# Second block's attention: the order in which differential and grouped pairs of a query tile are worked

## The reference, cut to what matters

```python
def _diff_attention(dq, dk, dv, lam):
    s = jnp.einsum('bqhjd,bkhjd->bhjqk', dq, dk).astype(jnp.float32) * ATTN_SCALE
    p = jax.nn.softmax(s, axis=-1)
    a = (p[:, :, 0] - lam * p[:, :, 1]).astype(dv.dtype)
    return jnp.einsum('bhqk,bkhe->bqhe', a, dv)

def _gqa_attention(gq, gk, gv):
    s = jnp.einsum('bqhgd,bkhd->bhgqk', gq, gk).astype(jnp.float32) * ATTN_SCALE
    p = jax.nn.softmax(s, axis=-1).astype(gv.dtype)
    return jnp.einsum('bhgqk,bkhd->bqhgd', p, gv)
```

## Time and profile before

| what | us |
|---|---|
| median of 3 runs | 4246.14 (4244.86 to 4246.96) |
| the profiled execution | 4247.18 |
| its span in the trace | 4245.3 |
| attention of layer 0 in the trace | from 1516 to 1711 |
| attention of layer 1 in the trace | from 3237 to 3397 |
| TensorE busy over the span | 3767.7 (89%) |
| VectorE, ScalarE, GpSimd busy over the span | 1764.2, 864.0, 1032.4 |

### The profile page before, as it was taken

The page is one execution under the profiler, slowest core; times in us unless marked ns, Lnnn a source line. Parts: engine busy times, 40 slices in busy tenths (PEclk is TensorE's granted clock), DMA queues, the critical chain, the costliest instruction groups (busy, mean ns, idle before and its releaser), DMA issues. The chain is left out here.

```text
span 4245.3 us, 46759 instructions
## 1 busy us (share of the span) xinstructions
PE 3767.7 (89%) x17898; PEld 2594.1 (61%) x17898; DVE 1764.2 (42%) x3243; ACT 864.0 (20%) x1654; POOL 1032.4 (24%) x866
## 2 busy tenths in 40 slices
PE   6967968777669989899998899999899989989998
PEld 5856735444455557555554455555687757767887
DVE  3345320000032256488643666654224635234345
ACT  2123320000031246211212100001223511221001
POOL 1301200000003410123332323232142024434443
PEclk9978989999879999999999999999999999999999
DMA  5430179999811100122221223221111012222221
GB/s 197 179 97 16 61 285 397 394 398 397 342 40 56 45 21 1 50 81 93 79 96 60 80 104 115 100 98 60 35 62 38 1 61 77 82 80 70 90 80 60
DMA packets 79787, 496.39 MB, mean 117 GB/s; under 512 B 9680, under 2 KB 11088, under 8 KB 25808
## 3 DMA queue, kind: packets, MB, share of 16 engines
q1 hardware_dynamic: 69920, 469.80, 29.7%
q0 software_dynamic: 3792, 12.85, 1.0%
q10 hardware_dynamic: 5856, 10.75, 0.7%
HBM read 476.58 MB, written 16.78 MB: 116 GB/s over the span
## 5 line engine op out<-in xcount | busy, mean ns | idle before, releaser
L1942 PE MATMUL ps<-expert_weights,experts_x_turned 128*64 128x256 f32 x2112 | 284.5, 430 | 89.7 <-DMA expert_weights<-w_moe 88.0
L1942 PEld LDWEIGHTS ps<-expert_weights,experts_x_turned 128*64 128x64 f32 x2112 | 199.4, 155 | 183.2 <-issue 127.7
L755 PE MATMUL ps<-projected,weight_ring 128*128 128x384 f32 (+1 forms) x672 | 245.8, 521 | 0.0
L2025 DVE TENSOR_TENSOR experts_hidden<-experts_silu_gate,ps 128x256 f32<-128x256 f32 x33 | 13.9, 421 | 493.0 <-PE ps L1942 493.0
L755 PEld LDWEIGHTS ps<-projected,weight_ring 128*128 128x128 f32 x672 | 127.7, 190 | 106.1 <-issue 45.9
L2952 PE MATMUL ps<-h2b,weight_ring 128*128 128x384 f32 (+1 forms) x512 | 153.5, 444 | 23.6 <-PEq L247 23.6
L1169 DVE TENSOR_REDUCE attention_shift<-ps 128x1 f32<-128x768 f32 (+1 forms) x160 | 130.9, 845 | 77.0 <-PE ps L1057 76.7
L2390 DVE SCALAR_TENSOR_TENSOR projected<-projected,sb_vectors 128x497 f32<-128x497 f32 (+26 forms) x270 | 157.8, 648 | 1.6
L1057 PE MATMUL ps<-projected 64*128 64x256 f32 (+1 forms) x576 | 135.8, 527 | 25.0 <-DVE projected L1198 15.0
L1908 POOL DMA_INDIRECT experts_gathered<-tokens,own_tokens x32 | 28.9, 902 | 517.9 <-PE ps L1930 455.4
L2250 PE MATMUL ps<-projected,gates_weight_sums 128*128 128x384 f32 (+1 forms) x512 | 149.1, 434 | 5.0 <-POOL gates_weight_sums L2530 5.0
(11 more groups left out here) (645 smaller groups left out, 7623.5 us busy)
## 6 DMA issues: line engine op xcount, KB each, us to landing
weight_ring<-w_stream SPq DMA_DIRECT2D x218, 1024.0 KB, 5.1
expert_weights<-w_moe SPq DMA_DIRECT2D x198, 1024.0 KB, 27.6
slot_out<-experts_down_out ACTq DMA_DIRECT2D x66, 128.0 KB, 7.5
weight_ring<-w_stream SPq DMA_DIRECT2D x16, 512.0 KB, 3.7
weight_ring<-w_stream SPq DMA_DIRECT2D x16, 384.0 KB, 3.1
slot_out<-sb_constants SPq DMA_DIRECT2D x15, 256.0 KB, 5.0
sb_x_all<-xT SPq DMA_DIRECT2D x1, 3072.0 KB, 12.2
tokens<-h_tokens ACTq DMA_DIRECT2D x4, 512.0 KB, 4.6
```

Of the source, the lines that this page charges most:

```text
L755: ins = nc.tensor.matmul(core.ps[:, 2 * slot + half, 0:n], w_of(k), h_of(k)[:, a:a + n], start=(first and k == 0), stop=(last and k == chu ...
L1942: ins = nc.tensor.matmul(out[OWN * j:OWN * (j + 1), :], x_t[:, k, :], w[j][:, k, :], start=(k == 0), stop=(k == KD - 1), skip_group_check= ...
```

## The change

One line is taken out: the second `for c in range(4):`. The body of the second loop now stands in the first, so that the list holds differential 0, grouped 0, differential 1, grouped 1, and so on, in place of four of one kind and then four of the other.

```diff
                     for c in range(4):
                         pairs.append({
                             "maps": [(pr[r:r + HD, DQ + c, q], pr[r:r + HD, DK + c, :]) for r in (0, HD)],
                             "diff": True, "keys": keys, "spans": [(0, keys)],
                             "v": lambda i, c=c: dv[:, i, c * P:(c + 1) * P],
                             "out": pr[:, DQ + c, q]})
-                    for c in range(4):
                         pairs.append({
                             "maps": [(pr[r:r + HD, GQ + c, q], pr[r:r + HD, GK + c // 2, :])
                                      for r in (0, HD)],
                             "diff": False, "keys": keys, "spans": [(0, keys)],
```

## The result

The changed kernel takes **4261.69 us** (median of 9 runs, 4252.91 to 4264.94) against 4246.96 us for the kernel before in the same session (9 runs, 4239.38 to 4249.96). The ratio is 1.0031, with a 95% interval of 1.002 to 1.0041. The change makes the kernel slower by about 0.3%. The forecast was 4252.2 with a range that ended at 4257.2, so the time lies above the range.

A forecast was written before the change was run, and what follows sets the result against it. TensorE's own chain was taken to set the pace in the long pairs. Layer 1's +2.9 and layer 0's +3.2 gave +6.1 us, hence 4252.2 us, with a range of 4246.7 to 4257.2.

The forecast's parts named there:

- Start of a layer: First pairs of each layer's attention: T0 of pair 1 waits for a copy, +1.4 us in layer 1, +1.0 in layer 0.
- The link itself: Layer 0's start: T0 of pair 1 waits for the copy of pair 0's T, taken as +1.0 us.
- layer 1: start: T0 of layer 1's pair 1 waits for the copy of pair 0's T: +1.4 us, between 0.7 and 2.3.
- layer 1: long tiles: Alternating long pairs in layer 1: two pairs take 9.60 us, +1.2 a layer, between 0.8 and 1.9.
- layer 1: end: Layer 1's last pairs: T of differential pair 30 waits for its mix uncovered, +0.3 us, between -0.2 and +0.6.
- layer 0: start: Layer 0's first short pairs: the same wait for a copy, with less to copy, +1.0 us, between 0 and 1.4.
- layer 0: seam short to long: Layer 0, first long pairs: T0 of the grouped pair waits for a copy, +0.7 us, between 0.3 and 0.8.
- layer 0: short tiles: Layer 0's 16 short pairs: alternation taken as 0, with 1.6 us either way.
- The alternation fills the waits: Long tiles: rival in which TensorE's 0.47 us waits go, 15.0 us saved, 4237.2 us; chance 0.04.
- VectorE becomes the bound: Steps with two copies and a mix: rival in which VectorE's scale comes late, some 4260 us; chance 0.11.
- ring: Long tiles: one differential and one grouped pair repeat on TensorE, 9.60 us for the two.
- Nothing to be seen: Whole kernel: rival in which changes to and from `gv` cost nothing and starts are hidden, 4246.1 us; chance 0.07.

The follow-up runs named there:

- filled: Matmuls of the identity, results unread, added at the start of each layer's attention; on the kernel before 4250.91 and 4247.74 us, against 4246.89 and 4246.57 without.
- the first tile alone: Alternation only in layer 0's first short tile, against the kernel before: 4254.67 against 4249.08 us, again 4253.38 against 4246.57.
- the three comparisons: The whole change against the kernel before, measured three times: 4261.69 against 4246.96 us, 4256.84 against 4248.26, 4258.16 against 4249.08.
- the crossed runs: Alternation in layer 0's first tile without (4253.38 us) and with extra start matmuls (4248.94), beside the kernel before (4247.74) and the change (4255.52), both with them.
- the filled change: The full alternation with extra identity matmuls at each layer's start, against the kernel before without them: 4252.25 against 4246.89 us, again 4255.52 against 4246.57.
- the filled kernel before: The order of before with extra identity matmuls at each layer's start, against the kernel before without them: 4250.91 against 4246.89 us, again 4247.74 against 4246.57.
- two and two: Two differential then two grouped pairs in all tiles, against the kernel before: 4245.95 against 4246.89 us, ratio 0.9994.
- the long tiles of layer 0 alone: Alternation only in the four long tiles of layer 0, against the kernel before: 4248.04 against 4248.26 us, ratio 0.9999.

## Why the prediction was wrong

**The step that failed is "Start of a layer", the sentence "Layer 0 starts with short pairs, with less to copy: I take +1.0, between 0 and 1.4".** The link itself was right: filled, the first tile's alternation costs 0.75 in the trace (197.07 - 196.32) and 1.6 +- 0.8 in the runs. But the prediction held the length of the low stretch fixed. It looked at the granted clock at layer 1's start only, where it asked what one T0 would cost at the lower level, and put the clock aside with "the granted clock in the long pairs is full already". For the short pairs at layer 0's start no row of the clock was read at all. There the alternation does not only run under a given low clock, it goes with a longer stretch of it. In full: the wait for the copy was taken as the whole cost of the start, and the clock under which all the pairs after it run was put at nothing. As measured, the first tile alone costs 6.0 +- 0.8 in place of 1.0, so the term was too small by about 5. With 5 more the sum would have been 11.1, near the +10.6 +- 0.9 that the three comparisons give together.

Some of the miss in the number is chance. The first comparison, +13.0, was the highest of the three; +10.6 on 4246.14 would be 4256.7, just inside the range that ended at 4257.2. But the range reached so far only by adding up all its upper bounds, and the bound of this term was 1.4. Of a slowdown beyond 8.5 us the prediction said 0.13, nearly all of it for a late VectorE, which no trace shows.

Does the sum now close? The three comparisons of the change with the kernel before gave +13.0 +- 1.9 (the result), +9.7 +- 1.1 and +10.6 +- 2.3, weighted +10.6 +- 0.9. The links at the full clock give 5.7 by the traces, and what the first tile costs beyond its link is 6.0 - 0.75 = 5.2 +- 0.8 by the runs: 10.9. The whole is met within its error, the split less well. That 4.4 +- 1.1 of the first tile's 6.0 goes away with the extra work, under which the clock is full, is shown by the crossed runs. That the low stretch carries all of it is not, since 7 us more of it, by the clocks of all executions, are worth about 2. The two stages of the three traces of the changed order lie 6.1, 9.6 and 5.5 us above those of before, 7.1 on average and not 10.6. And the sum leaves out layer 1's clock: its stage is 161.2 on average in the six unfilled traces in the order of before and 163.1 in the four that alternate, 1.9 more in place of the 3.1 at the full clock. So a remainder of 1 to 3 us either way isn't excluded.

**The other steps**, each at its measured size:

| term | predicted | measured at the full clock |
|---|---|---|
| layer 1: start | +1.4 | +1.75 (5.44 - 3.69, filled) |
| layer 1: long tiles | +1.2 | +1.13 (134.33 - 133.20) |
| layer 1: end | +0.3 | +0.23 (11.13 - 10.90) |
| layer 1: whole stage | +2.9 | +3.1 (163.0 - 159.9, filled) |
| layer 0: start | +1.0 | +0.75 (filled); 6.0 +- 0.8 by the runs, unfilled |
| layer 0: seam short to long | +0.7 | +0.61 (4.68 - 4.07) |
| layer 0: short tiles | 0 | -0.2 (filled, at the scale of pair 13) |
| layer 0: whole stage | +3.2 | +2.6 (198.88 - 196.32, filled) |
| both layers | +6.1 | 5.7 by the traces, 6.1 +- 0.7 by the runs, filled |

For the short tiles: the scale of pair 13 comes 39.99 us after the sums of lambda in the filled change, 40.17 with the first tile alone alternating, and 39.42 in the filled kernel before, so the second short tile takes back 0.2.

The start of layer 1 came out 0.3 too low: the old start was read from rows that partly ran at the lower clock (the scores after T are 2.50 long there, and 1.89 in the filled kernels), the new one was added up from rows at the full clock. The links as a whole were right within 0.4, with errors of both signs, and still the time came out above the range: a chain can be summed well and still leave out what sets the speed of its members.

**The rivals.** *The alternation fills the waits* fell: 0.48 still stands ahead of the scores at 1600.67 and at every second group after. *VectorE becomes the bound* fell: scale 1.54 behind the values, ring 9.59, and from the scale of pair 8 to that of pair 43 the three traces of the changed order take 156.01, 156.06 and 156.01. *Nothing to be seen* fell: the filled kernels, which differ in nothing but the order, lie 6.1 +- 0.7 apart, and their stages 5.7. The place where a loss beyond the sum was looked for, VectorE in the step with copies and mix, was the wrong one; it was the lower clock, and that was no rival at all.

**The price of changing between `gv` and `dv`.** The Trainium skill (TensorEngine Tiling (Array Packing), Tiling Modes, Key Properties) says that a change of the tiling mode drains TensorE. The traces agree in that `gv` stands 0.91 behind its transposition where `dv` stands 0.82, and T0 1.46 behind `gv` where it stands 1.33 behind `dv`, and they give the size for a tile: 2 x (9.60 x 2 - 18.96) = 0.5 us between the alternating order and two and two, which differ in which of the links are bare. That the cause is a drain is not shown: a group of `gv` also holds twice the matmuls of one of `dv` (x24 against x12 in the rows), and no run kept the width and changed the count.

**What stays open.** Why the low stretch is longer with alternating short pairs is only argued: TensorE waits there 0.67 for a copy at 1521.43, which the order of before does not have. That wait by itself does not bring the low clock, since it is there in the filled change too (1525.96) at the full clock, and it is not needed for a stretch of 14 us, which two kernels have whose first tile is in the order of before. No run took it away by itself. That extra work shortens the stretch to nothing in five traces of five with ten matmuls ahead of the lambda sums is shown; which of the waits decides is not. Nor is it known why the long tiles of layer 0 alone measured 0.0 +- 1.4, with a stage of 201.9 in the trace. The times of single executions spread around their mean by a standard deviation of 1.4 to 5.8 us, mostly 3 to 4, so one trace says little on a difference of this size.

## What to carry to other kernels

Before summing links of a chain, read the granted clock of each stretch that the new order touches, the short ones at a stage's start above all: a price read from rows at one clock holds for the new order only if the clock there is the same, and in all executions, not in the one that was profiled. Here it was neither at layer 0's start (a term of 1.0 that measured 6.0) nor at layer 1's (1.4, and 1.75 at the full clock). To take the clock out of a comparison of two orders, give both the same extra matmuls at the stage's start and compare these two with each other; here this brought 10 us down to a difference that the sum explains. What is left unsettled by that is whether the extra matmuls cost anything themselves, so such kernels are compared with each other only. What a change between two kinds of work costs depends on which links stand bare, not on how often the kinds change.

## What the runs showed of the hardware that I had not expected

The time that TensorE stays at its lower level at the start of layer 0's attention differs from execution to execution of the same order by 7 to 22 us (14 and 21 in the changed kernel, 21 and 43 with the first tile alone), and with it the stage of one and the same kernel took 203.3 and 211.2 us. The Trainium skill (TensorE: Matmul & The Clock Gate, A second HAM failure mode: psum-queue depth-cycling) tells of a bf16 kernel in which short idle times between groups of matmuls let the clock swing between its levels. The rows here fit only in part. The first tile alone has 0.47 idle ahead of every second group of scores at a granted clock of 0.52, but the changed kernel has 0.48 in the same places at 1531.69 and 1536.25 with the clock full: these waits alone do not tell which level it is.

Ten matmuls that compute nothing used, 2.47 us of TensorE's time ahead of the lambda sums, with a few more at pair 2, went with the full level from the first pair on in all five traces, and the stage of layer 0 fell from 197.7 to 196.3. That this made no faster kernel can be read from the traces. In layer 0 the lambda sums start 1.10 after VectorE's last work on the projection in the kernel before (1513.56 to 1514.66) and 3.18 after it in the filled one (1516.05 to 1519.23), so the extra work puts them off by 2.1, more than the 1.4 it gives back. In layer 1 it puts them off by 2.1 too, and the stage fell from 162.4 to 159.9 against the traces of before with the longer low stretch, while against those with the shorter (159.7 to 160.2) it is about the same.
